# Suffix sums of a stick-breaking attention folded to 64 rows on POOL, one pass of ones per key block, and squares of q and k on ScalarE

## The reference, cut to what matters

```
z        = (q k^T) / 8,  q and k RMS-normalised per head
log_1m   = where(key < query, log_sigmoid(-z), 0)
after    = reverse cumulative sum of log_1m over the keys, without the key's own
a        = where(key < query, exp(log_sigmoid(z) + after), 0)
out      = a @ v
```

## Time and profile before

| | |
|---|---|
| median of 3 runs | 1675.31 us (1673.73 to 1675.38) |
| the profiled execution | 1674.12 us |
| its span | 1672.4 us |
| PE busy | 1664.4 us (100%) |
| DVE, ACT, POOL busy | 947.6, 752.5, 180.0 us |
| TensorE clock granted | 0.999 of full |

### The profile page before, as it was taken

One profiled execution on the slowest core, in us unless ns is written; L12 is line 12 of the kernel. 1 busy time (PEld: TensorE's weight loads), 2 busy tenths in 40 slices (PEclk: granted clock), 3 DMA queues, 4 the chain that ended last, 5 costly groups with the idle time before them and its releaser, 6 DMA issues.

```text
span 1672.4 us, 22054 instructions
## 1 busy us (share of the span) xinstructions
PE 1664.4 (100%) x7608; PEld 1386.0 (83%) x7608; DVE 947.6 (57%) x1170; ACT 752.5 (45%) x1059; POOL 180.0 (11%) x171
## 2 busy tenths in 40 slices
PE   9999999999999999999999999999999999999999
PEld 7888888888888888888888888888888888888887
DVE  6887876545454434434649877765555444344344
ACT  7677676333342222223456777763333432232231
POOL 1333311000010000000123242200001100000000
PEclk9999999999999999999999999999999999999999
DMA  5222222333323223223333222223223222233233
GB/s 190 91 75 87 88 85 74 92 97 100 100 95 101 90 99 100 93 96 100 113 127 101 63 88 88 88 70 100 95 92 109 88 101 95 94 100 99 90 100 126
DMA packets 49154, 162.20 MB, mean 97 GB/s; under 512 B 5713, under 2 KB 5969, under 8 KB 49105
## 3 DMA queue, kind: packets, MB, share of 16 engines
q1 hardware_dynamic: 46656, 157.34, 28.8%
q10 hardware_dynamic: 2448, 4.23, 0.7%
HBM read 155.26 MB, written 2.10 MB: 94 GB/s over the span
## 4 chain that ended last, share of the span: by engine, by line
PE 94%; DVE 2%; ACT 1%; DVEq 1%; POOLq 0%; POOL 0%; issue 0%; DMA 0%; ACTq 0%; SPq 0%
PE bank L503 28%; PE bank L504 28%; PE bank L507 28%; PE z L576 2%; PE z L504 1%; PE z L507 1%; PE z L503 1%; PE z L549 1%; PE misc L592 1%; PE misc L590 1%; PE z L550 1%; DVE S L1314 0%; DMA xT<-in_x 0%; DVE N L1195 0%; DVE S L1312 0%
## 5 line engine op out<-in xcount | busy, mean ns | idle before, releaser
L503 PE MATMUL bank<-xg_hi,w_hi 128*128 128x512 f32 x1584 | 621.2, 392 | 0.0
L504 PE MATMUL bank<-xg_lo,w_hi 128*128 128x512 f32 x1584 | 616.8, 389 | 0.0
L816 ACT ACTIVATE w_hi<-raw 128x1024 fp32r<-128x1024 f32 (+1 forms) x294 | 303.5, 1035 | 481.4 <-DMA raw<-in_w_units 480.4
L1183 DVE TENSOR_TENSOR w_lo<-raw,w_hi 128x1024 fp32r<-128x1024 f32 (+1 forms) x294 | 370.1, 1262 | 41.1 <-ACT w_hi L816 22.3
L507 PE MATMUL bank<-xg_hi,w_lo 128*128 128x512 f32 x1584 | 392.1, 389 | 0.0
L507 PEld LDWEIGHTS bank<-xg_hi,w_lo 128*128 128x128 f32 x1584 | 297.3, 188 | 62.2 <-DVE w_lo L1183 0.2
L503 PEld LDWEIGHTS bank<-xg_hi,w_hi 128*128 128x128 f32 x1584 | 297.4, 188 | 61.7 <-issue 0.7
L504 PEld LDWEIGHTS bank<-xg_lo,w_hi 128*128 128x128 f32 x1584 | 297.5, 188 | 61.3 <-issue 0.7
L1188 DVE TENSOR_TENSOR S<-bank,rstd 128x512 f32<-128x512 f32 x152 | 104.9, 690 | 267.3 <-PE bank L507 266.6
L503 PE MATMUL bank<-mid_hi,w_hi 128*128 128x512 f32 x474 | 184.6, 390 | 0.0
L504 PE MATMUL bank<-mid_lo,w_hi 128*128 128x512 f32 x474 | 184.4, 389 | 0.0
(11 more groups left out here) (194 smaller groups left out, 1664.8 us busy)
## 6 DMA issues: line engine op xcount, KB each, us to landing
raw<-in_w_units SPq DMA_DIRECT2D x278, 512.0 KB, 3.3
raw<-in_w_units SPq DMA_DIRECT2D x20, 256.0 KB, 2.9
xT<-in_x SPq DMA_DIRECT2D x8, 256.0 KB, 6.3
mix_hi<-yb_hi ACTq DMA_DIRECT2D x8, 256.0 KB, 2.3
mix_lo<-yb_lo ACTq DMA_DIRECT2D x8, 256.0 KB, 2.4
out_x<-xT SPq DMA_DIRECT2D x7, 256.0 KB, 3.7
ln_g<-in_sgu_ln_g SPq DMA_DIRECT2D x2, 256.0 KB, 4.3
ln_b<-in_sgu_ln_b SPq DMA_DIRECT2D x2, 256.0 KB, 5.0
```

The lines of the kernel that those rows point to most:

```text
L503: mm(dst[:, :], wh[:, k0 + k, :], his[k], start=(k % per == 0), stop=False)
L504: mm(dst[:, :], wh[:, k0 + k, :], los[k], start=False, stop=False)
L816: af(w_hi[at.slot(c)][:, 0:kc, :], raw[at.slot(c)][:, 0:kc, :], ACT.Copy).then_inc(hi_done, 1)
L1183: tt(w[:, 0:kc, :], r[:, 0:kc, :], h[:, 0:kc, :].bitcast(F32), ALU.subtract).then_inc(lo_done, 1)
```

## The change

suffix on POOL is replaced. ACT, after softplus_hi, copies rows 64 to 127 of t_s (blocks 1 and 3+2) to rows 0 to 63 of two tiles of 384 columns (fold_halves). POOL adds rows 0 to 63 of t_s to them, so that each column sum needs 64 rows only, adds block 3 to block 2, adds that to block 1, rounds both tiles in rows 0 to 63 and writes the rests into rows 64 to 127. cumulate takes one pass of ones per block over the tile whose halves are hi and lo. The tiles lie in parts of yc, ya, gates, sq_hi, QT and KT that are free at the time; the last pair uses a second set.

In the three looped pairs head_square moves from POOL to ACT (two squares) and DVE (square_lo): on ACT that of q behind the rounding of v, that of k behind the first rms_chain; on DVE behind split_lo(4) and behind the norm of q. POOL then has only suffix, suffix, k_rest in a pair.

```diff
-            def suffix(h3):
-
-                pool.wait_ge(sp_ok, h3 + 3)
-                t2 = S_AT[2]
+            def suffix(h3, nth, tiles):
+
+                hl0, hl12, f0, f12 = tiles
+                half, other = slice(0, HD), slice(HD, P)
+                pool.wait_ge(fold_up, nth + 1)
                 pool.sem_inc(passed, 1)
-                nc.gpsimd.tensor_copy(suf[:, 0:P], t_s[:, t2:t2 + P])
-                nc.gpsimd.tensor_tensor(suf[:, P:2 * P], t_s[:, t2 + P:t2 + 2 * P], t_s[:, S_AT[3]:S_AT[3] + P], ALU.add)
+                nc.gpsimd.tensor_tensor(f12[half, :], f12[half, :], t_s[half, S_AT[3]:1280], ALU.add)
+                nc.gpsimd.tensor_tensor(f0[half, :], f0[half, :], t_s[half, S_AT[1]:S_AT[3]], ALU.add)
                 pool.drain()
-                nc.gpsimd.tensor_copy(suf_hi[:, :], suf[:, :])
+                nc.gpsimd.tensor_tensor(f12[half, 2 * P:], f12[half, 2 * P:], f12[half, 0:P], ALU.add)
                 pool.drain()
-                nc.gpsimd.tensor_tensor(suf_lo[:, :], suf[:, :], suf_hi[:, :].bitcast(F32), ALU.subtract
-                                        ).then_inc(suf_ok, 1)
+                nc.gpsimd.tensor_tensor(f0[half, P:], f0[half, P:], f12[half, P:], ALU.add)
                 pool.drain()
+                nc.gpsimd.tensor_copy(hl12[half, :], f12[half, :])
+                nc.gpsimd.tensor_copy(hl0[half, :], f0[half, :])
+                pool.drain()
+                nc.gpsimd.tensor_tensor(hl12[other, :], f12[half, :], hl12[half, :].bitcast(F32), ALU.subtract)
+                nc.gpsimd.tensor_tensor(hl0[other, :], f0[half, :], hl0[half, :].bitcast(F32), ALU.subtract)
+                pool.drain()
+                pool.sem_inc(suf_ok, 1)
...
-                    suffix(h3)
-                    head_square(l * 8 + (j * 2 + 3), QT)
-                    head_square(l * 8 + (j * 2 + 4), KT, m + 2)
-                    suffix(h3 + 3)
+                    suffix(h3, l * 8 + j * 2, folds)
+                    suffix(h3 + 3, l * 8 + (j * 2 + 1), folds)
                     k_rest(l * 8 + (j * 2 + 4))
...
-                parts = [(s_hi, suf_hi), (s_lo, suf_lo)]
                 for g, blocks in Z_BLOCKS:
                     for i in blocks:
-                        for s, u in parts:
-
-                            terms = [(neg_tri, s, S_AT[i], i)]
-                            if i == 0:
-                                terms.append((neg_ones, s, S_AT[1], 1))
-                            if i < 2:
-                                terms.append((neg_ones, u, 0, 2))
-                            if i == 2:
-                                terms.append((neg_ones, s, S_AT[3], 3))
...
+                        at, width = Z_AT[i], T - P * i
+                        for s in (s_hi, s_lo):
+                            last = mm(z[g][:, at:at + width], neg_tri[:, :], s[:, S_AT[i]:S_AT[i] + width],
+                                      start=False, stop=(s is s_lo and i == 3), skip_group_check=True)
+                        if i < 3:
+                            last = mm(z[g][:, at + P:at + width], neg_ones[:, :], later[i],
+                                      start=False, stop=True, skip_group_check=True)
...
+            def fold_halves(tiles):
+
+                for f, a in ((tiles[3], S_AT[3]), (tiles[2], S_AT[1])):
+                    last = af(f[0:HD, :], t_s[HD:P, a:a + 3 * P], ACT.Copy)
+                last.then_inc(fold_up, 1)
+
+            def head_square(n_raw, src):
+
+                act.wait_ge(qk_raw, n_raw)
+                act.sem_inc(passed, 1)
+                af(S2[:, :], src[:, :], ACT.Square)
+                af(sq_hi[:, :], src[:, :], ACT.Square).then_inc(qk_sq_hi, 1)
...
                     softplus_hi(h3)
+                    fold_halves(folds_last if last else folds)
...
                     af(v_both[:, :, 0, :], misc[:, :].rearrange("p (n c) -> p n c", c=HD), ACT.Copy).then_inc(v_hi_ok, 1)
+                    if not last:
+                        head_square(l * 8 + (j * 2 + 3), QT)
...
                     rms_chain(nch, misc, HD, misc_free)
+                    head_square(l * 8 + (j * 2 + 4), KT)
...
                     softplus_hi(h3 + 3)
+                    fold_halves(folds)
...
+            def square_lo(nth):
+
+                dve.wait_ge(qk_sq_hi, nth + 1)
+                dve.sem_inc(passed, 1)
+                tt(sq_lo[:, :], S2[:, :], sq_hi[:, :].bitcast(F32), ALU.subtract).then_inc(qk_sq, 1)
```

## The result

| | before | after |
|---|---|---|
| median | 1674.76 us | 1732.76 us (1729.89 to 1735.17, 4 runs) |
| ratio | | 1.0349 (1.0336 to 1.0362) |
| span of the profiled execution | 1672.4 us | 1733.4 us |
| TensorE clock granted | 0.999 | 0.983 |
| PE busy | 1664.4 us (100%) | 1679.6 us (97%) |

What follows compares the result with a forecast made beforehand. TensorE's matmuls were taken to bound the kernel. From 1674.1 us, 11.1 of removed work and sq_lo waits went off and 45.6 of new waits came on: 1708.6, rounded to 1709, range 1681 to 1730.

Steps and rivals of the forecast that it cites:

- What bounds the kernel: TensorE's matmuls fill the span, PE waits only 5.5 us; matmul columns removed shorten the kernel one for one.
- What the change removes: In cumulate 16 matmuls become 11, 0.61 us a head, 9.8 us; with PE's sq_lo waits, 1.3 us, gain 11.1 us.
- the rival of a saving that isn't there: In cumulate, narrow passes bound by weight loads take away at most 9.8 us of gain; chance 0.05.
- The squares moved for nothing: Squares of q and k fit ACT's idle time in the pairs at no cost; without that cover 7.5 us more.
- The chain on POOL: Suffix ahead of cumulate: POOL's eight operations, drains and semaphore take 6.1 us alone, 7.1 by the upper ends.
- The locks: During the suffix each DVE operation with two SBUF inputs adds its length once; cumulate waits 1.7 to 5.9 us.
- the half-lock rival: DVE's operations fall into POOL's drains or come too late; cumulate waits shrink 1.3 us in 14 places: 1691; chance 0.20.
- Attend: At second attends attention_lo may end late, as k_rest meets the convolution; PE waits 0.2 us, 6 times, 1.2 us.
- The clock: Rival: waits at cumulate bring back 1.2 GHz, 1.2 us each in up to 14 places, 17 us: 1726; chance 0.15.
- The rival that ends on the other side: The suffix is done in time for cumulate; only pair 0 waits, 2 x 2.3 us: 1667.6; chance 0.08.

Runs made afterwards that it cites:

- no additions: The changed kernel without POOL's four additions in the suffix, so its attention is not right and it serves for time alone; 1674.8 us, ratio 1.0004.
- fold first: The changed kernel with ACT's two fold copies ahead of softplus_hi, in second heads of looped pairs also ahead of split_hi(7); 1721.73 us, ratio 1.0283.
- DVE's work moved: The changed kernel with DVE's w_lo of units 3 and 4 and square_lo behind the scaling of KT in the looped pairs; 1707.25 us, ratio 1.0191.
- the fold alone: The changed kernel with the squares of q and k left on POOL between its two suffixes as before; 1735.43 us, ratio 1.0368.

## Why the prediction was right in sign and too small

**What bounds the kernel.** Right. The table above has terms of PE's time only, and it closes.

**What the change removes.** Right: 0.65 us a head measured (2.27 to 1.62), 0.61 forecast; the sum is 10.4 for 9.8. So the rival of a saving that isn't there is out. The waits on sq_lo gave 1.7 us for 1.3, for their hidden part.

**The squares moved for nothing.** Right; two runs of their own show it.

**The chain on POOL.** Right in range: alone 6.66 us, forecast 6.1 to 7.1 with 6.1 taken. The operations lay at the upper ends of what was forecast for them: 384 columns 1.0 us, 256 0.73, 128 0.46, the copies 0.50. 64 rows are indeed no faster than 128: 128 columns take 0.46 us with either.

**The locks.** Right in kind, and the half-lock rival is out. Laid out by hand the waits came to 44.4 us without attend's share; 47.0 were measured. Head by head: pair 0 5.9 forecast and 5.89, 5.87 measured; first heads of pairs 1 and 2 3.4, and 3.33 to 3.45; second heads 2.6, and 2.38 to 2.55. That the first heads agree to a tenth is partly luck: POOL's own work was 0.6 us longer than taken and the window 0.5 us shorter (6.2 for 6.67, of which 0.3 were forecast), and the locks 0.8 us shorter. The one that was mis-sized is the last pair's first head, 1.7 against 3.41 and 3.50: I had counted two w_lo there, but a third, that of the next unit, meets POOL's last subtraction, which takes 1.97 us there as it does in pair 1, and the window was 6.2 us for the 6.6 taken.

**Attend.** 0.2 us six times was forecast, nothing was shown, because the longer waits at cumulate cover it. Without them it was 1.3 each (no additions), 0.9 to 2.0 (fold first). The cover was named; the size of what it covers wasn't seen, and its cause was not k_rest at the convolution, which was there before, but ACT's copies and POOL's work ahead of it.

**The clock.** This is the step that failed: the slow clock behind PE's waits was a rival with a small chance and had no term in the sum, and it cost 24.0 us. The prediction priced it at 1.2 us from the stretch 9 to 12 us and gave it a chance of 0.15, with the reason that "each of these waits stands behind 16 us and more of dense matmuls". That reason fell: the dense work ahead did not keep the clock. Behind every wait of 3 us and more it went to the lower level, in the changed kernel for 5.2 to 6.4 us of work each time. And the price was read from a stretch of 3 us at the kernel's start, cut without regard to where the slow period ended; a whole one behind these waits costs 3.0 us. The number of places was too high in turn: 8, not 14, as the shorter waits did nothing in this run. Together 24.0 us; with 3.5 of hidden waiting that is about the whole of what was missing, 26.6 us in the profiled execution. With the clock at its right price the forecast sum would read 1674.1 - 11.1 + 45.6 + 24.0 = 1732.6. That this is the median measured is luck in part: the sum has no hidden waiting, and the profiled execution, from which the 24.0 come, took 1735.2. The Trainium skill, TensorE: Matmul & The Clock Gate, Part 1, has it that the throttled clock is the default which activity releases; by that rule a wait in the middle of a kernel can bring it back as well as one at its start, and the traces here agree, at eight waits of the changed kernel.

**The rival that ends on the other side.** Faster, 1667.6, if the suffix were in time. It is out for this kernel. But it is also worth less than it seemed: with a suffix nearly in time in every pair (no additions) the kernel took 1674.8, since DVE becomes late for attend. The chance of 0.08 was reasoned from the locks alone.

**What stays open.** What decides, at a wait between 2 and 3 us, whether the clock falls. In the pairs of the changed kernel and eight variants it fell behind all 27 waits of 3.0 us and more, behind 19 of 44 between 2.0 and 2.7, and behind none of 16 between 1.3 and 2.0. It is not the code around the wait: with DVE's work moved, the second heads waited 2.4 to 2.5 us six times, and it fell twice. No run here isolates what else enters.

## What to carry to other kernels

On a kernel whose PE is full, price a new wait of PE as its shown length, a quarter of a microsecond that the idle time hides, and the clock behind it: here 1.5 to 3.2 us (once 4.3) for each wait above 3 us and for some above 2, with 16 us and more of dense matmuls ahead; where a wait can't be avoided, put matmuls that are due anyway in front of it, since even useless ones paid. Work taken off PE and given to POOL pays only where the window holds POOL's operations end to end with every two-input operation of DVE that falls between them: lay out both queues head by head and judge each place by itself; here one of the eight heads of a layer had the room. Before an operation is moved out of such a window, look at whose window it moves into.

## What the hardware showed that was not expected

- The granted clock fell from 1.00 to 0.50 in the middle of the kernel, after tens of microseconds of dense matmuls. It was back 2.9 to 6.4 us after it fell or, where it had fallen during the wait, after the wait's end (once, with the fold alone, after some 8.6). In several places it fell only a microsecond after the wait was over.
- POOL's one-input copies are held back by DVE too: a cast of 64x384 took 0.50 us alone, 0.79 beside DVE's square_lo in the changed kernel and 1.50 beside w_lo with the fold first.
- Ninety-six useless matmuls made the kernel 15 us faster.
